# Two attention turns written out apart from the loop, and new sums copied before the last gates

## What is computed

```
z    = (q . k) * HD**-0.5 + bias                         # logits
u    = where(mask, log_sigmoid(-z), 0)
rev  = cumsum(u, reverse=True) - u
A    = where(mask, exp(log_sigmoid(z) + rev), 0)          # s < t strictly
out  = A @ v
```

## Time and profile before

| | |
|---|---|
| time, median of 3 runs | 1483.4 us (1479.48 to 1486.56) |
| time of the profiled execution | 1485.67 us |
| its span, first to last instruction | 1483.7 us, so 2.0 us lie around it |
| PE busy | 1440.4 us, 97% |
| DVE, ACT, POOL busy | 77%, 51%, 26% |
| mean granted TensorE clock | 0.993 |
| DMA | 222.63 MB, 150 GB/s over the span |

### The profile page before, as it was taken

How to read it: one execution, slowest core, us unless ns; L and a number is a source line. 1 busy time by engine, 2 the same in 40 slices (tenths; PEclk the granted TensorE clock), 3 DMA queues, 4 the chain that set the end, 5 groups by cost and what they waited for, 6 DMA issues and landing times.

```text
span 1483.7 us, 32623 instructions
## 1 busy us (share of the span) xinstructions
PE 1440.4 (97%) x12792; PEld 1366.2 (92%) x12792; DVE 1145.0 (77%) x1847; ACT 763.5 (51%) x1168; POOL 382.3 (26%) x435
## 2 busy tenths in 40 slices
PE   8999999999999999999999599999999999999998
PEld 8999999999999999998998487778899999999998
DVE  7866666667898988989944667777689989898753
ACT  6544444435663645546541355665656546464543
POOL 4000000002322323322144434443332332323221
PEclk9999999999999999999999899999999999999999
DMA  6133333222677786786527878986337778778621
GB/s 193 58 89 89 88 88 88 88 88 79 132 175 165 153 194 152 163 185 143 129 87 226 245 235 276 270 262 185 125 85 153 173 159 183 156 161 188 142 86 65
DMA packets 247958, 222.63 MB, mean 150 GB/s; under 512 B 12364, under 2 KB 228500, under 8 KB 247828
## 3 DMA queue, kind: packets, MB, share of 16 engines
q1 hardware_dynamic: 157490, 155.74, 34.3%
q0 software_dynamic: 72256, 55.59, 22.4%
q10 hardware_dynamic: 18082, 9.48, 2.3%
HBM read 192.19 MB, written 11.80 MB: 137 GB/s over the span
## 4 chain that ended last, share of the span: by engine, by line
PE 80%; DVE 7%; DMA 5%; issue 4%; SPq 2%; ACT 2%; DVEq 0%; POOL 0%; ACTq 0%; POOLq 0%
PE acc L2830 22%; PE acc L3154 17%; PE pL L3154 12%; PE pMO L3154 11%; PE acc L3254 3%; DMA wraw<-in_w_down_dram 2%; DMA Kp<-in_cache_k_dram 2%; SPq L540 2%; PE pL L2951 1%; DVE KX L2496 1%; PE pMO L3325 1%; PE acc L3091 1%; PE pMO L3020 1%; PE acc L3362 1%; PE acc L3512 1%
## 5 line engine op out<-in xcount | busy, mean ns | idle before, releaser
L676 POOL TENSOR_TENSOR wlo<-wraw,whi 128x512 fp32r<-128x512 f32 x40 | 55.7, 1422 | 449.3 <-ACT whi L805 449.3
L2830 PE MATMUL acc<-xa_hi,whi 128*128 128x288 f32 x544 | 125.1, 311 | 0.6 <-issue 0.6
L891 ACT ACTIVATE hi<-wraw 128x1024 fp32r<-128x1024 f32 x60 | 63.7, 1062 | 111.8 <-DVE wraw L2013 111.8
L2830 PE MATMUL acc<-xa_hi,wlo 128*128 128x288 f32 x544 | 116.5, 296 | 0.0
L2830 PE MATMUL acc<-xa_lo,whi 128*128 128x288 f32 x544 | 116.1, 295 | 0.0
L874 ACT ACTIVATE hi<-wraw 128x1024 fp32r<-128x1024 f32 x60 | 63.7, 1061 | 99.9 <-PE acc L3154 99.7
L3154 PE MATMUL acc<-X_lo,hi 128*128 128x288 f32 x384 | 113.3, 295 | 0.0
L3154 PE MATMUL acc<-X_hi,lo 128*128 128x288 f32 x384 | 113.3, 295 | 0.0
L3154 PE MATMUL acc<-X_hi,hi 128*128 128x288 f32 x384 | 113.2, 295 | 0.0
L2028 DVE TENSOR_TENSOR lo<-wraw,hi 128x1024 fp32r<-128x1024 f32 x60 | 73.3, 1222 | 40.4 <-ACT hi L874 40.2
L3154 PE MATMUL acc<-H_hi,hi 128*128 128x288 f32 x336 | 99.3, 296 | 1.3 <-DVE lo L2034 1.3
(11 more groups left out here) (512 smaller groups left out, 4965.5 us busy)
## 6 DMA issues: line engine op xcount, KB each, us to landing
wraw<-in_w_up_dram SPq DMA_DIRECT2D x64, 512.0 KB, 6.8
wraw<-in_w_down_dram SPq DMA_DIRECT2D x64, 512.0 KB, 5.9
Kp<-in_cache_k_dram SPq DMA_DIRECT2D x32, 512.0 KB, 4.7
Vp<-in_cache_v_dram SPq DMA_DIRECT2D x32, 512.0 KB, 5.5
wraw<-in_w_in_a_dram SPq DMA_DIRECT2D x30, 512.0 KB, 5.0
wraw<-in_w_up_dram POOLq DMA_DIRECT2D x32, 256.0 KB, 4.9
S_even<-in_w_up_dram POOLq DMA_DIRECT2D x32, 256.0 KB, 7.2
S_odd<-in_w_up_dram POOLq DMA_DIRECT2D x32, 256.0 KB, 7.6
```

Of the source, the lines that this page charges most:

```text
L676: ins = pool.tensor_tensor(wlo[s][:, k:k + 2, :], wraw[s][:, k:k + 2, :], whi[s][:, k:k + 2, :].bitcast(F32), ALU.subtract)
L891: act.activation(blocks4(hi31), by_depth(G % 2)[:, 0], ACT.Copy).then_inc(piece_hi, 1)
L2830: last = pe.matmul(acc[a][:, hf, 0:HALF], w[s][:, k, a * P:(a + 1) * P], x[k][:, hf * HALF:(hf + 1) * HALF], start=(k == 0 and n == 0), st ...
```

## The change

Four things are done.

1. **Turn 1 leaves the loop** and gets a form between turn 0 and the loop (`late`): `keys_turned(j + 1, 2)` and `(j + 1, 3)` move from the start of the turn to its middle, around `mask(j, 2)`, `past_logits(j + 1, 0)` on PE moves from behind `fill(0, 2)` to behind `fill(2, 5)`, `past_logits(j + 1, 1)` from behind `fill(5, 8)` to behind `fill(9, 13)`, and ACT's `past_gates(j + 1)` behind `q_high(j + 1)`.
2. **In turn 0** `keys_turned(1, 0)` moves ahead of the turn, `keys_turned(2, 0)` and `(2, 1)` move from behind `weights(0, 1, 1)` to behind `q_low(1)`, and ACT's `kv_split(1, 1)` moves from ahead of `gates(0, 1)` to behind `new_copies(0)`.
3. **On SP** the value pages of sequence 0 go ahead of its second moves, the first three key pages of sequence 1 go between them and `keys_moved(1, 0)`, and in every turn `kv_weights(j + 2, 1)` goes behind the two key pages.
4. **In every turn** `new_copies(j)` goes ahead of `gates(j, 2)` on ACT.

Nothing that is computed changes. The diff, cut to its core:

```diff
@@ SP, pages_and_weights
                 keys_moved(j + 1, 1)
                 if j < NPAIR - 2:
-                    kv_weights(j + 2, 1)
                     key_page(j + 2, 0)
                     key_page(j + 2, 1)
+                    kv_weights(j + 2, 1)
@@ SP, before the turns
                 kv_weights(1, a)
+            sp.wait_ge(unit_done, U_OB)
+            value_pages(0)
+            keys_moved(0, 1)
             key_page(1, 0)
             key_page(1, 1)
-            sp.wait_ge(unit_done, U_OB)
-            keys_moved(0, 1)
-            value_pages(0)
+            key_page(1, 2)
             keys_moved(1, 0)
-            key_page(1, 2)
             key_page(1, 3)
@@ ACT, pair
                 v_rows(j)
-                if first:
-                    kv_split(1, 1)
                 gates(j, 1)
                 at_copy(j, 0)
                 at_copy(j, 1)
+                new_copies(j)
+                if j == 0:
+                    kv_split(1, 1)
                 gates(j, 2)
-                new_copies(j)
                 weights_in(0)
-                if not first:
+                if not late:
                     past_gates(j + 1)
                 at_copy(j, 2)
                 k_high(j + 1)
                 at_copy(j, 3)
                 q_high(j + 1)
-                if first:
-                    past_gates(1)
+                if late:
+                    past_gates(j + 1)
@@ DVE, pair
                 mask(j, 0)
                 if first:
-                    keys_turned(1, 0)
                     keys_turned(1, 1)
                 else:
                     past_store(j)
+                if not late:
                     keys_turned(j + 1, 2)
                     keys_turned(j + 1, 3)
...
                 products(j, 1, 0)
-                if first:
-                    keys_turned(1, 2)
+                if late:
+                    keys_turned(j + 1, 2)
                 mask(j, 2)
-                if first:
-                    keys_turned(1, 3)
+                if late:
+                    keys_turned(j + 1, 3)
                 products(j, 1, 1)
                 kv_copy(j + 1, 0)
                 weights(j, 1, 0)
                 weights(j, 1, 1)
-                if more:
+                if more and not first:
                     keys_turned(j + 2, 0)
                     keys_turned(j + 2, 1)
...
                 q_low(j + 1)
+                if first:
+                    keys_turned(2, 0)
+                    keys_turned(2, 1)
@@ DVE, before the turns
             kv_copy(0, 1)
+            keys_turned(1, 0)
             dve.wait_ge(row_chain, 3)
...
             pair(0, True, True)
-            with dve.Fori(1, NPAIR - 2) as j:
+            pair(1, True, True)
+            with dve.Fori(2, NPAIR - 2) as j:
@@ PE, pair
                 if first:
                     past_transposed(0)
-                else:
+                elif not late:
                     past_logits(j + 1, 0)
...
                 if first:
                     past_finish(0)
+                elif late:
+                    past_logits(j + 1, 0)
...
                 fill(5, 8)
-                if not first:
+                if not late:
                     past_logits(j + 1, 1)
...
                 fill(9, 13)
-                if first:
-                    past_logits(1, 1)
+                if late:
+                    past_logits(j + 1, 1)
```

More of the change, by code:

```diff
@@ L1459, in past_AT, with pair @@
                 act.activation(ATp[:], TB, ACT.Copy).then_inc(AT_done, 1)
-            def pair(j, weights_in, first=False):
+            def pair(j, weights_in, late=False):
                 k_rows(j)
-                if first:
+                if j == 0:
                     past_AT(0)
@@ L1525, in _ @@
             pair(0, lambda a: kv_split(2, a), True)
-            for j in range(1, NPAIR - 2):
+            pair(1, lambda a: kv_split(3, a), True)
+            for j in range(2, NPAIR - 2):
                 pair(j, lambda a: kv_split(j + 2, a))
@@ L2631, in ob_low, with pair @@
                                   ).then_inc(x_ready, 1)
-            def pair(j, first, more):
+            def pair(j, late, more):
+                first = late and j == 0
                 mask(j, 0)
                 if first:
-                    keys_turned(1, 0)
                     keys_turned(1, 1)
@@ L3368, in past_finish, with pair @@
                 pe.transpose(ZB[:, 2 * P:3 * P], Oc[:], ident[:]).then_inc(fin_full, 1)
-            def pair(j, first):
+            def pair(j, late):
                 def fill(k0, k1):
                     kv_fill(j + 1, k0, k1)
+                first = late and j == 0
                 keys_transposed(j)
@@ L3486, in _ @@
             pair(0, True)
-            with pe.Fori(1, NPAIR - 1) as j:
+            pair(1, True)
+            with pe.Fori(2, NPAIR - 1) as j:
                 pair(j, False)
```

## The result

The changed kernel takes 1487.0 us (median of 7 runs, 1486.3 to 1491.0) where the kernel before takes 1482.2 beside it: ratio 1.0035, interval 1.0022 to 1.0048, **5 us slower**. The prediction was 1483.1. The profiled execution took 1488.05 with a span of 1486.1; before it was 1485.67 and 1483.7.

A forecast was written before the change was run, and what follows sets the result against it. PE at work was taken as the bound, apart from turn 0's stalls, set by a chain of pages, transposes and moves. Turn 0 8.8 us earlier, mostly lost in turn 1: 1483.4 - 0.3 = 1483.1 us, range 1474.5 to 1490.

The forecast's parts named there:

- New copies ahead of the gates: 0: Loop turns: moving the new copies ahead of the gates on ACT changes the time by 0.
- The rival: Loop turns: POOL, ready inside DVE's first product, goes in before the second; 1488 to 1492 us, chance 0.23.
- The price: Loop turns: DVE's loss to POOL, 1.3 us seen once, 2.2 at worst; over turns 2 to 5 +5.2 to +8.6.
- Three waits: Turn 0: PE's waits of 2.49 (DVE's product), 3.45 (new tokens' copies) and 5.30 us (prompt's last weights) go.
- The one for the moves: Turn 0: PE's wait for moves of past keys, 3.88 us, stays and grows to 5 to 7; they land at 842.0.
- The tail: Turn 0: from the moves' landing at 842.0 to the start of turn 1, 11.7 us.
- the term for the clock: Turn 0: PE's product with the values takes 3.2 us, between 2.40 at full clock and 4.14.
- the sum of both turns: Turns 0 and 1 together: -0.3 us, tail bounds -2.1 and +0.7; with turn 0's landing bounds -4 and +3.
- The chain: Turn 0: one chain of key pages, transposes and moves sets its end; DVE waited 12.73 us for sequence 2's pages.
- "The moves land as soon as they are issued": Turn 0: moves issued by about 834.5 land at 838, turn 1 starts at 850; 1475 to 1479 us, chance 0.20.
- "The front end collides": Front: value pages before sequence 0's second moves push turn 0 back 1.5 to 3 us; up to 1489.5, chance 0.12.

The follow-up runs named there:

- run 5: The kernel before, unchanged, run once more as a kernel of its own; ratio 0.9999 (0.9986 to 1.0011), turn 0 50.24 us.
- run 2: The kernel before with only new_copies(j) put ahead of gates(j, 2) in turns 1 to 6; ratio 1.0040 (1.0025 to 1.0054), +5.9 us.
- run 1: The changed kernel with the new copies put back behind the last gates in turns 2 to 6; ratio 1.0020 (1.0007 to 1.0034), median 1485.2 us.
- Runs 9 and 11: 9: run 1 with key pages ahead of the moves in turn 1, 1.0013; 11: the kernel before with pages ahead of the moves in turn 0, 1.0006.
- run 8: Run 1 with SyncE's order at the front as in the kernel before; ratio 1.0020 (1.0010 to 1.0030).
- run 13: Run 1 with turn 1 back in the loop in its normal form on ACT, DVE and PE; ratio 0.9995 (0.9985 to 1.0005).
- run 3: The changed kernel with ACT's split put behind past_gates(j + 1) from turn 2 on, copies still early; ratio 1.0038 (1.0023 to 1.0053).

## Why the prediction was wrong

**The loop turns: "New copies ahead of the gates: 0" is the step that failed.** I had looked for who waits for the gates and copies on ACT, and nobody does. What the move changed is when ACT reaches the split, and so when POOL is ready. The rival named it, with its place and the point from which it decides (878.54 against 878.25), and I took the forecast, with that margin of 0.3 us as a reason. It went over: in each of turns 2 to 6 the two products take 2.37. Against the same turns of run 5 (29.3 to 29.4, and 28.8 for turn 6) the changed kernel loses 1.1 us in each of turns 3 to 5, 0.5 in turn 6, and 1.8 in turn 2, where a late key page (0.62 at 909.98) is in it too. The sign that the prediction named for this, a loop turn of 30.5 with a product over 1.3 us beside POOL, came. The price was put at 1.3 to 2.2 a turn. The second product ran for 1.77 instead of 0.67, so the size was the one POOL instruction that got in, not both. Run 2 shows the step alone at 5.9 us, run 1 the return of the products to 1.28. The Trainium skill (SBUF — State Buffer, Who interferes with whom) says that a DVE instruction with two SBUF inputs contends with a GpSimd one that reads SBUF, and that the order of issue decides who blocks; by that rule the time would be that of this rival, and the trace agrees, at each loop turn, while a scan in turn 0 doesn't fit it (last section).

**Turn 0: right in which waits go, short in size.** Turn 1 was forecast to start at 853.7, between 851 and 856, and did at 850.1. Turn 0 itself was to be 8.8 shorter and was 13.6. Three waits went as written. The one for the moves was to grow to 5 to 7 and fell from 3.88 to 1.69, for one of 3.17 for a product came ahead of it that was not written: PE reached it early, and DVE had waited for a key page and had scans beside POOL's split ahead of it. The moves landed at 840.5 and not 842.0, ahead of its bounds of 841.0 to 842.8. The tail was at full clock, 9.5 from 840.6 to the next turn where 11.7 was written; the term for the clock (3.2 for the product with the values) should have been 2.40, and the past logits 1.07 and not 1.94.

**Turn 1: right in place, short in size.** DVE waited 6.8 and 2.1 us for key pages (6 to 9 forecast), PE 6.9 (some 5, with 4 to 6 as the sign). From the end of the transposes to turn 2 it took 12.2, as written. What was not in it: POOL's split beside a scan, 3.00 us at 852.81 instead of 1.18, a lead for the wait of 1.71 at 866.34; no run took it away alone. Turn 2 started at 890.4, forecast 891.6: in the profile the sum of both turns was right within its bounds.

**The chain: named, but one link was missed.** The prediction had pages, transposes and moves. It took the pages for the late link. Runs 9 and 11 show the moves out of the single `KX` right behind them: in the changed kernel's turn 1 the last move landed at 872.6 and the page was turned at 873.6, in turn 0 of the kernel before at 844.5 and 846.9. No repair of one link gained. And the base was one execution with a turn 0 of 51.3. By the ratios, the change without the loop's copies did not gain 0.3 but lost 3.0 (runs 1 and 8, uncertain by 2.0 and 1.5). One trace of each, run 1 against run 5, has the loss not in turns 0 and 1 (78.8 against 79.9) but behind them, in turns 2 and 3 (61.2 against 58.7), by the late key pages. Split up, the copies cost 2.2 us on top of the rest (1.0035 to 1.0020, uncertain by 2.8), turn 1's late form 3.7 (1.0020 to 0.9995, by 2.5), and the rest gives 0.7 (by 1.5): of the parts only the late form stands clear of zero in this split, and the copies in run 2.

**The other rivals.** "The moves land as soon as they are issued" did not happen: 5.5 us at the median for SyncE's between 833 and 838. "The front end collides" neither: a wait of 1.1 at 811.4, within its bound of 0 to 2, and run 8 finds no price for that order.

Open is why turn 0 differs by 3 us between executions of one kernel, and why in run 1 the pages of turns 2 and 3 came late; by run 8, where they didn't, it is not the loop's order alone.

## What to carry to other kernels

An instruction that is moved on one engine also moves the start of what that engine releases: list what runs side by side on two engines that were seen to make each other wait (here DVE and POOL), with the margins, and treat a margin of 0.3 us as lost. The moment when such an instruction becomes ready can hang on another engine than the one that was reordered (run 13: PE). If a stall reappears one turn later after each repair, look for a chain of reused buffers, count its links, and see which of them come due at the same time before repairing the one that is seen to wait. If issues are moved behind one another in one queue, count the time of issuing too: what stands behind them starts later. Before a single trace serves as the base of a sum, see how far its execution is from the median and from where.

## What the runs showed of the hardware that I had not expected

- A scan with two inputs in SBUF loses to POOL as a product does. In turn 0 of the changed kernel, DVE and POOL:
```profile
833.15 3.58 DVE L2590 TENSOR_TENSOR_SCAN pg<-fg,ones 128x255 f32<-128x255 f32 x1
...
833.66 2.52 POOL L756 TENSOR_TENSOR wlo<-wraw,whi 128x512 fp32r<-128x512 f32 x2
```
  Such a scan takes 0.6 alone (two in 1.27). The 32x32 transposes have a single input and lost nothing to speak of beside the same split (2.36 in run 3 and 2.37 at 879.10, where the two at 815.11 of the kernel before took 2.37 with POOL idle).
- In the loop turns, who waits is decided between two products of DVE that stand back to back: a split that is ready inside the first gets in before the second. POOL lost too, 3.17 for its two instead of 2.5. This is how the products of the loop turns behave, and no rule for all: the scan above had begun 0.51 us before POOL's split and still waited for both of its instructions.
- How many POOL instructions DVE waits for varies: one in the loop (1.77 for 0.67), two at 833.15 and at 821.96. What decides it is open.
- The same moves of 64 KB land in 2.4 us or 7.0, by what was issued ahead of them.
